# Two transformer blocks in split float32: other places in SBUF for activations and split weights

## The reference, cut to what matters

```python
# first block, one layer
h = h + jnp.concatenate([attn, rec], axis=-1) @ w_out[l]
h = h + memory_cross_attention(rmsnorm(h, norm_cross_g[l]), rmsnorm(memf, norm_mem_g[l]), ...)
hid = jnp.square(jax.nn.relu(rmsnorm(h, norm_mlp_g[l]) @ w_mlp_in[l]))      # 1024 -> 4096
h = h + hid @ w_mlp_out[l]                                                  # 4096 -> 1024
...
# second block, two layers
x = x + merged @ w_out[l]
h2 = rmsnorm_2(x, ln_ffn[l])
g_part, u_part = jnp.split(h2 @ w_gate_up[l], 2, axis=-1)                   # 1024 -> 2 x 2816
x = x + (jax.nn.silu(g_part) * u_part) @ w_down[l]                          # 2816 -> 1024
```

## Time and profile before

| | before |
|---|---|
| median of 3 runs | 1294.37 us (1293.87 to 1296.36) |
| the profiled execution | 1295.53 us, span 1293.7 us |
| TensorE busy | 1265.9 us, 98% of the span |
| VectorE busy | 862.2 us, 67% |
| ScalarE busy | 652.5 us, 50% |
| mean DMA rate | 164 GB/s |
| granted TensorE clock | 0.994 of full speed |

### The profile page before, as it was taken

One profiled execution on the slowest core, in us unless ns is written; L12 is line 12 of the kernel. 1 busy time (PEld: TensorE's weight loads), 2 busy tenths in 40 slices (PEclk: granted clock), 3 DMA queues, 4 the chain that ended last, 5 costly groups with the idle time before them and its releaser, 6 DMA issues.

```text
span 1293.7 us, 22072 instructions
## 1 busy us (share of the span) xinstructions
PE 1265.9 (98%) x9208; PEld 1178.1 (91%) x9208; DVE 862.2 (67%) x1194; ACT 652.5 (50%) x1049; POOL 114.4 (9%) x152
## 2 busy tenths in 40 slices
PE   8999999999999999998999999999999999999998
PEld 8998999988788989997999998888899988999986
DVE  6897667644466675998656553667577996655543
ACT  5896655543368464342544443556552434544432
POOL 1100000000000000661000000000003810000000
PEclk8999999999999999999999999999999999999999
DMA  9543445555535323442555555433343325455552
GB/s 368 204 163 115 180 135 192 196 185 180 188 101 193 131 99 131 164 152 84 189 189 176 190 196 185 165 139 136 112 145 131 134 96 196 165 191 174 187 196 98
DMA packets 30324, 211.77 MB, mean 164 GB/s; under 512 B 3344, under 2 KB 3728, under 8 KB 5264
## 3 DMA queue, kind: packets, MB, share of 16 engines
q1 hardware_dynamic: 29936, 210.22, 45.5%
q10 hardware_dynamic: 288, 0.14, 0.0%
HBM read 209.29 MB, written 1.05 MB: 163 GB/s over the span
## 4 chain that ended last, share of the span: by engine, by line
PE 74%; DVE 13%; ACT 6%; issue 5%; DMA 1%; SPq 0%; DVEq 0%; ACTq 0%
PE bank L508 72%; DVE w_lo L1625 3%; ACT w_hi L1125 2%; DVE W L1599 2%; DMA ring<-weight_pieces 1%; ACT W L1125 1%; PE bank L608 1%; PE bank L843 1%; DVE xs L2125 1%; DVE W L1585 1%; DVE junk L2123 1%; DVE W L2105 1%; DVE W L1586 1%; DVE W L1617 0%; DVE stat L1558 0%
## 5 line engine op out<-in xcount | busy, mean ns | idle before, releaser
L1625 DVE TENSOR_TENSOR w_lo<-ring,w_hi 128x2048 fp32r<-128x2048 f32 x183 | 422.5, 2309 | 283.9 <-ACT w_hi L1125 283.5
L1125 ACT ACTIVATE w_hi<-ring 128x1024 fp32r<-128x1024 f32 (+1 forms) x368 | 366.2, 1046 | 241.9 <-PE bank L508 226.2
L508 PE MATMUL bank<-x_hi,w_hi 128*128 128x256 f32 x1840 | 267.2, 284 | 2.4 <-ACT w_hi L1125 2.4
L508 PE MATMUL bank<-x_hi,w_lo 128*128 128x256 f32 x1840 | 261.5, 281 | 1.0 <-DVE w_lo L1625 0.9
L508 PE MATMUL bank<-x_lo,w_hi 128*128 128x256 f32 x1840 | 254.8, 280 | 0.0
L508 PEld LDWEIGHTS bank<-x_hi,w_hi 128*128 128x128 f32 x1840 | 237.0, 189 | 5.7 <-issue 2.4
L508 PEld LDWEIGHTS bank<-x_hi,w_lo 128*128 128x128 f32 x1840 | 236.5, 188 | 2.3 <-DVE w_lo L1625 1.7
L508 PEld LDWEIGHTS bank<-x_lo,w_hi 128*128 128x128 f32 x1840 | 233.6, 188 | 0.0
L508 PE MATMUL bank<-W 128*128 128x128 f32 (+4 forms) x716 | 110.7, 327 | 8.3 <-ACT W L1125 4.8
L508 PEld LDWEIGHTS bank<-W 128*128 128x128 f32 (+3 forms) x716 | 87.8, 187 | 21.5 <-issue 12.3
L508 PE MATMUL bank<-w_lo,hid_hi 128*128 128x512 f32 x304 | 78.5, 394 | 0.0
(11 more groups left out here) (257 smaller groups left out, 1238.0 us busy)
## 6 DMA issues: line engine op xcount, KB each, us to landing
ring<-weight_pieces SPq DMA_DIRECT2D x191, 1024.0 KB, 4.8
const<-constants SPq DMA_DIRECT2D x1, 1376.5 KB, 8.9
W<-x_features SPq DMA_DIRECT2D x4, 256.0 KB, 5.2
ring<-weight_pieces SPq DMA_DIRECT2D x2, 512.0 KB, 6.0
h<-x SPq DMA_DIRECT2D x2, 512.0 KB, 11.9
W<-rg_weights SPq DMA_DIRECT2D x1, 1024.0 KB, 9.7
xs<-mem_features SPq DMA_DIRECT2D x1, 1024.0 KB, 11.4
oT<-mem SPq DMA_DIRECT2D x1, 1024.0 KB, 11.4
```

The source lines that it names most:

```text
L508: return nc.tensor.matmul(out, lhsT, rhs, start=first, stop=last)
L1125: return nc.scalar.activation(out, in_, ACT.Copy, scale=scale)
L1625: v.tensor_tensor(w_lo[:, q % SPLITS, 0:n], raw(pp)[:, 0:n], w_hi[:, q % SPLITS, 0:n].bitcast(F32), ALU.subtract).then_inc(s_weight_low, 1)
```

## The change

The activations become one tensor `x_hi_lo`, in which the high and the low part of a feature tile stand side by side (tiles 2048 bytes apart instead of 1024), and it comes first in SBUF. A view function `x_at(name)` shifts all of it by 24, 12 or 0 numbers: for the MLP input of the first block by 24 (6 lines), for the second MLP by 12 (3 lines), for the third and for everything else by 0. `w_hi` and `w_lo` become four tensors, one for each buffer, with a gap of 64 numbers (16 lines) ahead of those of odd pieces. Constants and gains move behind the arena. Every engine has the same instructions in the same order with the same waits; only addresses and names differ, so no rows of an order are shown.

Where the operands of split products start then, as (start of the stationary operand minus start of the moving one) in lines of 16 bytes, modulo 32:

| matmuls | count | before | after, even pieces | after, odd pieces |
|---|---|---|---|---|
| `up`, first MLP | 768 | 12 | 2 | 18 |
| `gu`, second MLP | 1056 | 12 | 5 | 21 |
| `gu`, third MLP | 1056 | 12 | 8 | 24 |
| other `feat` | about 2640 | 12 | 8 | 24 |
| `tok` (v, wout, b, c, hg) | about 1100 | 20 | 24 | 8 |
| down products, 512 columns | 912 | 20 | 16 | 0 |

```diff
+X_ROOMS = {"norm_mlp_g": 24, "ln_ffn_0": 12, "ln_ffn_1": 0}
+X_ROOM = max(X_ROOMS.values())
...
+        sb("to_a_line", [P, 2])
+        x_both = sb("x_hi_lo", [P, KT * 2 * S + X_ROOM], F32R)
+        sb("gap0", [P, 8])
         ring = sb("ring", [P, RING, PIECE])
-        w_hi = sb("w_hi", [P, SPLITS, PIECE], F32R)
-        w_lo = sb("w_lo", [P, SPLITS, PIECE], F32R)
-        const = sb("const", [P, C_SIZE])
-        vec = sb("vec", [P, V_SIZE])
-        row = sb("row", [P, R_SIZE])
         h = sb("h", [P, TT, D])
         xs = sb("xs", [P, TT, D])
-        x_hi = sb("x_hi", [P, KT, S], F32R)
-        x_lo = sb("x_lo", [P, KT, S], F32R)
         oT = sb("oT", [P, KT, S])
+        w_hi0 = sb("w_hi0", [P, PIECE], F32R)
+        w_lo0 = sb("w_lo0", [P, PIECE], F32R)
+        sb("gap1", [P, 64])
+        w_hi1 = sb("w_hi1", [P, PIECE], F32R)
+        w_lo1 = sb("w_lo1", [P, PIECE], F32R)
+        w_hi, w_lo = (w_hi0, w_hi1), (w_lo0, w_lo1)
+
+        def x_at(name=None):
+
+            room = X_ROOMS.get(name, 0)
+            v = x_both[:, room:room + KT * 2 * S].rearrange("p (k a t) -> p k a t", k=KT, a=2)
+            return v[:, :, 0, :], v[:, :, 1, :]
+
+        x_hi, x_lo = x_at()
         W = sb("W", [P, ARENA])
...
+        const = sb("const", [P, C_SIZE])
+        vec = sb("vec", [P, V_SIZE])
+        row = sb("row", [P, R_SIZE])
...
-                hi, lo = (w[:, q % SPLITS, 0:KT * n].rearrange("p (k c) -> p k c", k=KT) for w in (w_hi, w_lo))
+                hi, lo = (w[q % SPLITS][:, 0:KT * n].rearrange("p (k c) -> p k c", k=KT) for w in (w_hi, w_lo))
...
-                        gemm(job, "m", p, "feat", parts=parts, between=between)
+                        gemm(job, "m", p, "feat", parts, None, *x_at("norm_mlp_g" if name == "up" else f"ln_ffn_{l}"), between)
...
-                                    ins = copy(x_hi[:, k, :], bank[:, k % 2, :], gain[:, k:k + 1])
+                                    ins = copy(x_at(name)[0][:, k, :], bank[:, k % 2, :], gain[:, k:k + 1])
...
-                                ins = v.scalar_tensor_tensor(x_lo[:, k, :], bank[:, k % 2, :], gain[:, k:k + 1], x_hi[:, k, :].bitcast(F32), ALU.mult, ALU.subtract)
+                                ins = v.scalar_tensor_tensor(x_at(name)[1][:, k, :], bank[:, k % 2, :], gain[:, k:k + 1], x_at(name)[0][:, k, :].bitcast(F32),
+                                                             ALU.mult, ALU.subtract)
```

More of the change, by code:

```diff
@@ L514, in first_gemm @@
                 bank = fill(job, "g")
-                hi, lo = (w[:, 0, :].rearrange("p (k c) -> p k c", k=KT) for w in (w_hi, w_lo))
+                hi, lo = (w[0][:, :].rearrange("p (k c) -> p k c", k=KT) for w in (w_hi, w_lo))
                 for half, kh in ((0, 0), (0, 1), (1, None)):
@@ L533, in first_gemm, with gemm @@
                 last_job[p] = job
-            def gemm(job, group, p, form, n=256, parts=None, ks=None, x_hi=x_hi, x_lo=x_lo, between=None):
+            def gemm(job, group, p, form, parts=None, ks=None, x_hi=x_hi, x_lo=x_lo, between=None):
+                n = 256
                 q = split_of[p]
                 bank = fill(job, group)
-                hi, lo = (w[:, q % SPLITS, 0:KT * n].rearrange("p (k c) -> p k c", k=KT) for w in (w_hi, w_lo))
+                hi, lo = (w[q % SPLITS][:, 0:KT * n].rearrange("p (k c) -> p k c", k=KT) for w in (w_hi, w_lo))
                 pe.wait_ge(s_weight_high, 2 * q + 1)
@@ L709, in _ @@
                     elif name in ("up", "gu"):
-                        gemm(job, "m", p, "feat", parts=parts, between=between)
+                        gemm(job, "m", p, "feat", parts, None, *x_at("norm_mlp_g" if name == "up" else f"ln_ffn_{l}"), between)
                     elif name == "co":
                         q = split_of[p]
-                        hi, lo = (w[:, q % SPLITS, :].rearrange("p (k c) -> p k c", k=4) for w in (w_hi, w_lo))
+                        hi, lo = (w[q % SPLITS][:, :].rearrange("p (k c) -> p k c", k=4) for w in (w_hi, w_lo))
                         pe.wait_ge(s_weight_high, 2 * (q + 1))
@@ L736, in _ @@
                             for k in range(KT):
-                                ins = mm(bank[:, 0:S], w[:, q % SPLITS, 32 * k:32 * k + P], x[:, k, :], i == k == 0, i == 2 and k == KT - 1)
+                                ins = mm(bank[:, 0:S], w[q % SPLITS][:, 32 * k:32 * k + P], x[:, k, :], i == k == 0, i == 2 and k == KT - 1)
                         full(ins, job)
@@ L752, in _ @@
                         q = split_of[p]
-                        hi, lo = (w[:, q % SPLITS, :].rearrange("p (k c) -> p k c", k=2) for w in (w_hi, w_lo))
+                        hi, lo = (w[q % SPLITS][:, :].rearrange("p (k c) -> p k c", k=2) for w in (w_hi, w_lo))
                         if j == 0:
@@ L1143, in split_ahead @@
                         cut = slice(half * n // 2, (half + 1) * n // 2)
-                        copy(w_hi[:, q % SPLITS, cut], raw(pp)[:, cut]).then_inc(s_weight_high, 1)
+                        copy(w_hi[q % SPLITS][:, cut], raw(pp)[:, cut]).then_inc(s_weight_high, 1)
             act.dma_start(vec[:], vec_d).then_inc(s_vec, 16)
@@ L1208, in _ @@
                                 act.wait_ge(s_first_loaded[half], 16)
-                                copy(w_hi[:, 0, cut], raw(0)[:, cut]).then_inc(s_weight_high, 1)
+                                copy(w_hi[0][:, cut], raw(0)[:, cut]).then_inc(s_weight_high, 1)
                                 continue
@@ L1624, in split_ahead @@
                     dve.wait_ge(s_weight_high, 2 * (q + 1))
-                    v.tensor_tensor(w_lo[:, q % SPLITS, 0:n], raw(pp)[:, 0:n], w_hi[:, q % SPLITS, 0:n].bitcast(F32), ALU.subtract).then_inc(s_weight_low, 1)
+                    v.tensor_tensor(w_lo[q % SPLITS][:, 0:n], raw(pp)[:, 0:n], w_hi[q % SPLITS][:, 0:n].bitcast(F32), ALU.subtract).then_inc(s_weight_low, 1)
             def product_low(m):
@@ L1708, in _ @@
                             dve.wait_ge(s_weight_high, half + 1)
-                            v.tensor_tensor(w_lo[:, 0, cut], raw(0)[:, cut], w_hi[:, 0, cut].bitcast(F32), ALU.subtract).then_inc(
+                            v.tensor_tensor(w_lo[0][:, cut], raw(0)[:, cut], w_hi[0][:, cut].bitcast(F32), ALU.subtract).then_inc(
                                 (s_first_low, s_weight_low)[half], 1)
```

## The result

| | before | after |
|---|---|---|
| median of 18 runs each | 1294.85 us (1292.75 to 1298.18) | 1296.95 us (1295.11 to 1298.51) |
| the profiled execution | 1295.53 us, span 1293.7 | 1298.34 us, span 1296.5 |

The ratio is 1.0015, with an interval of 1.0009 to 1.0021. It excludes 1, so the kernel became slower, by less than the 0.2% at which the prediction draws its line. The forecast of 1289.7 us had the wrong sign; the time lies in the range.

What follows compares the result with a forecast made beforehand. TensorE's start-to-start matmul spacing was taken as the bound. The terms -8.2 + 3.1 + 0.4 = -4.7 us took the median of 1294.4 to 1289.7 us, range 1269 to 1306 us.

Steps and rivals of the forecast that it cites:

- Step 1: Whole kernel: instructions, waits, queues and DMA stay as before in the same order, cost 0.
- Step 2: Projections of first and second MLP, 1824 matmuls at 2, 18, 5 and 21: 113.3 ns each, 8.2 us gained.
- Step 3: Moving weights at 24 and 8: 672 matmuls of value, output and side projections lose the fast gait, 3.1 us lost.
- Step 4: Third MLP and all other moving activations, 3696 matmuls at 8 and 24: 117.9 for 117.8 ns, 0.4 us lost.
- Step 5: Down product, 912 matmuls at 16 and 0: stays at 233.3 ns, 0; bounds 18.3 us gained, 9.2 us lost.
- Step 6: Full fp32 matmuls and transposes: their distance changes too, but half the read rate hides such meetings, 0.
- Rival 1: Matmul spacing everywhere: restarts after stalls set the gaits, not addresses; 1294.4 us, within 2.6, chance 0.27.
- Rival 2: Down product's odd pieces at distance 0 cost 4.6 us, MLPs gain nothing, other projections lose; 1302.5 us, chance 0.26.
- Rival 3: MLP or down product: one distance avoids the meetings altogether, 106.6 or 213.2 ns a matmul; 1272.8 us, chance 0.14.

Runs made afterwards that it cites:

- The map: Three variants of the changed kernel with even and odd pieces at different distances and each MLP shifted separately: 1293.42, 1296.16 and 1296.53 us, one run each.
- all_at_4: Changed kernel with every activation view shifted by 56 numbers, so moving activations stand at distance 4 and moving weights at 12: 1285.26 us, ratio 0.9915.
- down_only: Kernel before with 48 numbers of room ahead of the arena W, down product at distance 0 instead of 4: 1287.37 us, ratio 0.9945.
- back_to_12: Changed kernel with views and weights shifted so moving activations are at 12 and moving weights at 4 again, down product at 0: 1288.61 us, ratio 0.9949.
- map_low: Changed kernel with even and odd pieces at 0 and 6, 1 and 7, 4 and 10 in the three MLPs, down at 6 and 0: 1293.42 us.

## Why the prediction was wrong

The mechanism was right as far as the forecast needs it: the change acts through the distance between the places of stationary and moving operand, and in the MLPs TensorE's spacing shows in full. Whether it is the two reads that meet, which the prediction called likely, no run showed. What the distances are worth was wrong, in three terms. The sizes below are sums of the distances from start to start in the two profiled executions.

- **Step 1, no instruction changes: holds.** Same counts and the same busy time on VectorE and ScalarE.
- **Step 2, first and second MLP at 113.3 ns because 2 and 5 lie next to 4 (-8.2 us): this is the step that failed.** Measured 118.3 and 119.3 ns, +0.4 and +1.5 us. The prediction named it as the weakest; it interpolated between places on a curve of which it had three points. The map shows that neighbours have nothing in common: 4 has 5.45 us a piece (or 5.65), 3 and 5 have 5.72. And 4 itself would not have been safe: with all three MLPs there, `all_at_4` stayed at 117.8 ns, so the 113.3 of the earlier trace rows was one of two gaits. That the distance counts modulo 16 was right: even and odd pieces are alike in all stages.
- **Step 3, moving weights lose the fast gait (+3.1 us): right.** From start to start they took 161.8 us instead of 158.9, +2.9.
- **Step 4, third MLP and others at 8 (+0.4 us): mis-sized.** The third MLP took 120.0 ns, +2.2 us; the others took 118.9 ns and lost 1.1 us in all. The bound of 118.8 ns, the slowest row there was, did not hold for the MLP, though the sum of 3.3 us stays under the bound of 3.7. The row of 117.9 ns from which this step took its size was not distance 8 alone: `mem_lo` lies 4 lines off `mem_hi`, so a third of the matmuls in it were at 12.
- **Step 5, down product unchanged (0): mis-sized.** Measured 226.7 ns, -5.7 us, inside the bounds of -18.3 to +9.2. `down_only` shows it by itself.
- **Step 6, full fp32 unchanged (0): holds where the traces tell.** The products of `oT` with `ring` went from distance 12 to 0 and start 214.3 ns apart in both kernels, holes left out.

The sum with measured sizes: +1.9 (step 2), +2.9 (step 3), +3.3 (step 4), -5.7 (step 5) make +2.4 us, and 2.8 were seen between the profiled executions; the rest is in the small products and their waits. Step 2 decides the sign: with +1.9 in the place of -8.2 and all else as predicted, the sum is +5.4 us and not -4.7. That the time came out only 2.1 us over the median before is the work of step 5, which was expected to give nothing.

**Rival 1** (addresses have no effect) is refuted: the time of a piece changes from one to the next with its buffer alone, and one gap takes 5.7 us off the down products. Its second half, that a start may set the gait, has something left for distance 4. Its number, 1294.4, was nevertheless nearer to the result than the forecast's, because gains and losses cancelled. **Rival 2** had the sign and half of its mechanism (no gain in the MLPs, steps 3 and 4); but odd pieces of the down product at distance 0 are not dearer, they are at the best place there is, as the even ones. **Rival 3** was right that a much better place exists, only it is 9, which the change doesn't use; and no place in any run went below 113.3 ns.

The Trainium skill states in "TensorE: Matmul & The Clock Gate" (section "Step-by-step: what each phase is for") that the moving and the weight read have ports of their own, so that a weight load takes nothing from a running matmul. By that rule places would have no effect, as the prediction worked out in rival 1. The runs here disagree: with the same instructions and the same clock, places alone move the spacing from 113.3 to 120.0 ns. The measurement decides; that it is the weight load that takes the time was only argued.

## What to carry to other kernels

When TensorE never idles and its matmuls still start further apart than their columns need, the places of the two operands in SBUF are worth a look: a gap of some 200 bytes gained 0.5% here, and the best places 1.4%, with no instruction changed. Don't interpolate between places: let two buffers of one kernel stand at different distances, so that one run compares them piece by piece, and then run the best one over the whole kernel, since a place can behave differently beside itself than beside another. And cost a change by start-to-start distances in each stage; a total of +0.15% here hid 5.7 us gained and 8.5 lost.

## What the runs showed of the hardware

- A matmul of 256 columns of `F32R` with its own weight load starts every 113.3 to 120.0 ns at the full clock, by the distance of the start lines (16 bytes) of its operands modulo 16; one of 512 columns every 226.7 to 234 ns. Interleaving the activations, splitting the weights into four tensors and moving all absolute places left 117.8 ns at distance 12 as it was (`back_to_12`); at distance 8 both 118.7 and 120.0 ns turn up in either layout.
- No piece in any of the 13 kernels went below 113.3 and 226.7 ns a matmul, one twice the other. Against the 106.6 that the low clock of the earlier trace rows suggests (213 ns / 2), that is about 17/16. What the last sixteenth is, no run told.
- Some distances (4, 7, 8, 14, 15) have two gaits. For 4, `all_at_4` has the slow one (117.8 ns) from the third piece on in every MLP and `map_low` the fast one (113.5) in all even pieces of the third but one. For 7, `map_low` has 5.60 and 5.70 us from one odd piece to the next. What chooses between them is open.
- Matmuls in full fp32 of 256 columns start 214.3 ns apart at distance 12 (before) and at 0 (after).
- Whether the reads of a matmul's own weights or those of the next ones meet the moving read was asked in two runs, and the answer was neither alone.
